# A decoder step on one core: the residual add of the last stage on GpSimd instead of VectorE

## The reference, cut to what matters

```
x = x + g2 * _apply_moe(h2, ...)
y = x * lax.rsqrt(jnp.mean(x * x, axis=-1, keepdims=True) + 1e-6) * final_g
```

## Time and profile before

| | us |
|---|---|
| median of 3 runs | 1414.49 (1413.54 to 1415.04) |
| the profiled execution, its own time | 1411.95 |
| its span in the profile | 1409.3 |
| PE, DVE, ACT, POOL busy in the span | 1237.8, 751.2, 509.1, 187.0 |
| last store of expert rows issued | 1354.03 |
| last stage, from its first load to the end of the span | 1357.96 to 1409.3 |

### The profile page before, as it was taken

The page is one execution under the profiler, slowest core; times in us unless marked ns, Lnnn a source line. Parts: engine busy times, 40 slices in busy tenths (PEclk is TensorE's granted clock), DMA queues, the critical chain, the costliest instruction groups (busy, mean ns, idle before and its releaser), DMA issues.

```text
span 1409.3 us, 18005 instructions
## 1 busy us (share of the span) xinstructions
PE 1237.8 (88%) x6859; PEld 946.1 (67%) x6859; DVE 751.2 (53%) x1417; ACT 509.1 (36%) x862; POOL 187.0 (13%) x169
## 2 busy tenths in 40 slices
PE   3688989899898899999999978996399998999956
PEld 1576767677675788888888867884367766666622
DVE  0665556645656452111111125445679887888827
ACT  1443232323324221111100112111178877878732
POOL 1110000000000000000000001110012253466301
PEclk8899999999999899999999999998589999999978
DMA  9442122231321121111111023223769999999644
GB/s 353 177 155 94 63 100 79 85 137 31 139 80 55 50 114 71 46 45 46 45 45 45 0 90 149 74 78 106 274 225 370 365 368 341 376 359 366 260 194 185
DMA packets 40717, 219.73 MB, mean 156 GB/s; under 512 B 7432, under 2 KB 15056, under 8 KB 27978
## 3 DMA queue, kind: packets, MB, share of 16 engines
q1 hardware_dynamic: 32194, 197.15, 37.5%
q0 software_dynamic: 7536, 18.51, 3.9%
q10 hardware_dynamic: 928, 3.28, 0.6%
HBM read 202.03 MB, written 24.72 MB: 161 GB/s over the span
## 4 chain that ended last, share of the span: by engine, by line
PE 62%; DVE 17%; DMA 14%; issue 3%; ACT 3%; SPq 1%; POOL 0%; ACTq 0%; POOLq 0%; DVEq 0%
PE p L1852 10%; PE p L1944 8%; DMA G<-in_we 8%; PE p L1619 7%; PE p L1856 6%; PE p L1789 3%; PE p L1879 3%; PE psS L1852 3%; PE psS L1879 3%; PE psS L1963 3%; DMA M<-in_x 2%; PE psS L1856 2%; DVE work L1150 2%; PE p L1686 2%; PE p L1697 1%
## 5 line engine op out<-in xcount | busy, mean ns | idle before, releaser
L1619 PE MATMUL p<-A 128*128 128x512 f32 (+3 forms) x1080 | 261.1, 389 | 14.3 <-DVE A L1047 14.3
L1619 PEld LDWEIGHTS p<-A 128*128 128x128 f32 (+1 forms) x1080 | 176.9, 185 | 66.8 <-DVE A L1047 16.2
L1944 PE MATMUL p<-C 128*96 128x512 f32 x768 | 195.0, 406 | 19.4 <-DVE C L1498 19.3
L1944 PEld LDWEIGHTS p<-C 128*96 128x96 f32 x768 | 122.5, 166 | 77.8 <-issue 30.3
L1487 DVE TENSOR_TENSOR C<-G,C 128x2048 fp32r<-128x2048 f32 x64 | 146.2, 2285 | 37.2 <-ACT C L907 37.2
L1302 DVE TENSOR_TENSOR work<-p,work 128x344 f32<-128x344 f32 x36 | 18.6, 517 | 238.4 <-ACT work L843 238.0
L1852 PE MATMUL p<-A,B 128*128 128x344 f32 x864 | 143.0, 323 | 2.0 <-DVE M L1236 2.0
L1852 PEld LDWEIGHTS p<-A,B 128*128 128x128 f32 x864 | 137.3, 188 | 4.4 <-issue 2.2
L907 ACT CAST C<-G 128x2048 fp32r<-128x2048 f32 x64 | 122.5, 1916 | 28.9 <-DMA G<-in_we 23.0
L1963 PE MATMUL psS<-C 128*96 128x512 f32 x384 | 98.3, 406 | 5.4 <-DVE C L1510 5.4
L627 POOL DMA_INDIRECT y_dram<-M,slotY x32 | 87.9, 2746 | 96.4 <-ACT M L936 96.4
(11 more groups left out here) (289 smaller groups left out, 1814.6 us busy)
## 6 DMA issues: line engine op xcount, KB each, us to landing
G<-in_we SPq DMA_DIRECT2D x32, 2048.0 KB, 18.3
G<-in_we SPq DMA_DIRECT2D x32, 1024.0 KB
M<-in_w_ada SPq DMA_DIRECT2D x8, 2048.0 KB, 8.0
M<-in_x SPq DMA_DIRECT2D x18, 512.0 KB, 4.2
M<-in_rope SPq DMA_DIRECT2D x45, 192.0 KB, 2.4
D<-in_w_qkv SPq DMA_DIRECT2D x4, 2048.0 KB, 7.8
F<-in_lift SPq DMA_DIRECT2D x8, 1024.0 KB, 5.1
M<-y_dram SPq DMA_DIRECT2D x8, 1024.0 KB, 11.9
```

The source lines that it names most:

```text
L1619: last = mm(out, x[k][:, t0:t0 + rows], y(k), start=k == 0 and j == 0, stop=k == KD - 1 and j == 2)
L1944: last = mm(up_bank[slot][0:CAP, :], x[:, k, :], kcols(w, k), start=k == 0 and j == 0, stop=k == KD - 1 and j == 2)
```

## The change

The add of the gated expert rows to the residual goes from DVE to POOL; DVE's `finish` follows two tiles behind `combine` instead of one; and `x2_r` is split. `x2_g` now counts gated tiles, which frees PE's banks and releases POOL's add; `x2_r` is counted by that add and still releases ACT's square. POOL's order is add(0), then add(t), rs3(t-1) for t = 1 to 8, then rs3(8); rs3(t) waits for finish(t-2), as `rstd3` has two columns. DVE's wait for its own halves in `combine` is gone. One semaphore, `modT_t`, is taken out and its step counted on `c_step` instead, with the same event and the same waiter, near the start of the program.

```
 CS = {... "cT_r": 4, "mod_t": 5}          # c_step counts modT_t's step too (DVE wait, PE inc)
@@ GpSimd
             def rs3(t):
                 pool.wait_ge(s["x2_sq"], t + 1)
+                if t >= 2:
+                    pool.wait_ge(s["yo_r"], t - 1)
...
+            def add_rows(t):
+                r = P if t < NT else NS
+                x = x1[0:r, t, :]
+                pool.wait_ge(s["x2_g"], t + 1)
+                nc.gpsimd.tensor_tensor(x, x, yg[0:r, t, 0], ALU.add).then_inc(s["x2_r"], 1)
             for t in range(NT + 1):
-                rs3(t)
+                add_rows(t)
+                if t:
+                    rs3(t - 1)
+            rs3(NT)
@@ VectorE
             def combine(t):
...
-                    link.mark(nc.vector.tensor_tensor(y0[:, cols], sum_bank[t % 3][n][0:r], gate[0:r, cols], ALU.mult))
-                link.wait()
-                nc.vector.tensor_tensor(x, x, y0, ALU.add).then_inc(s["x2_r"], 1)
+                    last = nc.vector.tensor_tensor(y0[:, cols], sum_bank[t % 3][n][0:r], gate[0:r, cols], ALU.mult)
+                last.then_inc(s["x2_g"], 1)
...
             combine(0)
-            for t in range(1, NT + 1):
+            combine(1)
+            for t in range(2, NT + 1):
                 combine(t)
-                finish(t - 1)
+                finish(t - 2)
+            finish(NT - 1)
             finish(NT)
@@ TensorE
                 if t >= 3:
-                    pe.wait_ge(s["x2_r"], t - 2)
+                    pe.wait_ge(s["x2_g"], t - 2)
```

More of the change, by code:

```diff
@@ L60 @@
 NL = NG + NE
-CS = {"c_sig": 1, "c_silu": 2, "cT_t": 3, "cT_r": 4}
+CS = {"c_sig": 1, "c_silu": 2, "cT_t": 3, "cT_r": 4, "mod_t": 5}
 SK = {"sq_t": 1, "sq_e": 2, "skT_t": 3, "skT_e": 5}
@@ L333, in build @@
         for n in ("const_in misc_in crow_in c_step ada_in0 ada_in1 ada_in2 ada_w "
-                  "ada_b ada_mm mod_r mod_st modT_t tab_in wq_in0 wq_in1 wq_hi wq_lo wq_free wkv_in kv_hi kv_lo x_in0 x_in1 x_in2 x_in3 rope_in0 rope_in1 x_n x_sq rs_r h_r "
+                  "ada_b ada_mm mod_r mod_st tab_in wq_in0 wq_in1 wq_hi wq_lo wq_free wkv_in kv_hi kv_lo x_in0 x_in1 x_in2 x_in3 rope_in0 rope_in1 x_n x_sq rs_r h_r "
                   "hT_t h_hi h_lo kv_mm k_r v_e kT_t kT_e pj rot v_c kd_r qk_t qk_e att_s nm_r ex_r pn_r pT_e st_u "
@@ L342, in build @@
                   "s2 hs h_a hid_r y_e y_st0 y_st1 y_st2 y_done wd_r ys_mm stab_in yg_in0 yg_in1 yg_in2 yg_in3 yg_in4 yg_in5 yg_in6 yg_in7 yg_in8 "
-                  "x2_r x2_sq rs3_r yo_r out_st0 out_st1").split():
+                  "x2_g x2_r x2_sq rs3_r yo_r out_st0 out_st1").split():
             sem(n)
@@ L1017, in _ @@
             link.wait()
-            dve.wait_ge(s["modT_t"], 1)
+            dve.wait_ge(s["c_step"], CS["mod_t"])
             parts = p2[:, :].rearrange("p (q j r) -> p j q r", q=4, j=4)
@@ L1559, in combine @@
                 gate = G2 if t < NT else G2s
-                y0, x = yg[0:r, t, 0], x1[0:r, t, :]
+                y0 = yg[0:r, t, 0]
                 for n in range(2):
@@ L1647, in _ @@
                 last = nc.tensor.transpose(p2[:, q * P:(q + 1) * P], mod[:, q * P:(q + 1) * P], ident)
-            last.then_inc(s["modT_t"], 1)
+            last.then_inc(s["c_step"], 1)
             kv(0)
```

## The result

The changed kernel takes 1420.22 us (median of 11 runs, 1416.63 to 1421.27), the kernel before 1413.54 (11 runs): ratio 1.0044, 95% interval 1.0036 to 1.0053, so 6.2 us slower (5.1 to 7.5). The forecast was 3.4 us slower, at 1417.9.

What follows compares the result with a forecast made beforehand. DVE was taken as the bound at 3.65 us a tile, PE close behind; POOL rounds of 4.10 us plus the tail end the last norm at 1407.9 instead of 1404.5, so 1414.49 + 3.4 = 1417.9 us, range 1412.8 to 1422.5.

Steps and rivals of the forecast that it cites:

- DVE just slower than PE, so little to win: Last stage: DVE takes 3.65 us a tile, PE 3.43, so relieving DVE can bring only 0.22 us a tile.
- Blocking both ways, one instruction against the other: Final norm and POOL's add, each reading two SBUF tensors, exclude each other; the norm holds the add 1.07 us.
- Gates are free of it: DVE's gates in the last stage read PSUM and one SBUF tensor, so POOL's add does not block them.
- POOL becomes the bound: Last stage: POOL's round is 0.03 + 1.07 + 2.1 + 0.90 = 4.10 us, 0.45 a tile slower than DVE before.
- DVE takes the port first: At each power's end, DVE's norm starts 0.03 us later, ahead of POOL's next add, and holds it 1.07 us.
- POOL gets the port first: Rival, chance 0.12: POOL's add starts before DVE's norm, which waits 2.0 us; rounds 4.5 to 4.6, time 1420.5.
- The first store is no wait any more: Norm 2 comes after tile 0's store has landed, so DVE's 1.9 us wait goes, without gain on the path.
- PE's loads wait for banks late in the stage: Sign: PE's loads stay at 0.43 us until its banks run out, then wait for gates late in the stage.

Runs made afterwards that it cites:

- the changed kernel again: The changed kernel, unaltered, run once more on the same chip as three other kernels: ratio 1.0032 to the kernel before.
- the fill: Kernel before, with POOL filling 128x2048 with zeros, reading nothing, behind each of the first eight powers: ratio 1.0001.

## Why the prediction was right

*DVE just slower than PE, so little to win.* Right. With the blocking gone and the add on POOL, rounds took 3.43 to 3.44 us, PE's pace, where DVE had set 3.65.

*Blocking both ways, one instruction against the other.* Right, and shown by experiments of its own. The sizes read from rows 6 and 7 hold: a norm holds POOL's add off for 0.97 to 1.04 us (1.07 taken), an add holds the norm off for 2.1 (2.0 taken).

*Gates are free of it.* Right: 684 ns in both kernels.

*POOL becomes the bound.* Right, with rounds of 4.46 instead of 4.10. The size was too small, 3.4 us against 6.2, and these terms made it so. The add takes 2.35 us, not the 2.1 that two passes of a copy would: 0.25 x 7 adds in a row (tiles 2 to 8; the power behind the add of tile 1 is still done just before gate 2) = 1.75 us. And the forecast gave every meeting to DVE. In fact the two orders take turns, 4.19 and 4.72 a round. By the forecast's terms with the measured add, a round would be 4.10 + 0.25 = 4.35; the average is 4.46, so 0.11 x 6 = 0.66 us more. Two errors lie in this 0.11: a round with DVE first measures 4.19, so its hand-over, hold and power were taken 0.16 too long (2.00 for 4.19 - 2.35 = 1.84), and the turns add 0.27 to it. In the profile with a short low clock, gate 2 was also done 0.3 us later after PE's start than forecast. Together 3.4 + 1.75 + 0.66 + 0.3 = 6.1, against 6.2 timed and 6.0 between the two profiles with a short low clock (47.6 - 41.6). (By the Trainium skill, GPSIMD Engine Reference, section 3.1 Elementwise, half of its 4497 ns at 2048 columns is an estimate of 2.25 us for the add, nearer than the 2.1 taken; the trace has 2.35.)

*DVE takes the port first.* Wrong as reasoned, and in half of the meetings right by luck. The forecast had the power release the norm and the add together, and the norm start first. Wherever the power does release both, it is the add that starts first, by 0.06 to 0.07 us (1382.61 against 1382.67, 1391.52 against 1391.59, 1400.43 against 1400.49): it stands right behind the power in POOL's own queue and starts before the power's row has ended, so the gap of 0.07 us that the forecast gave POOL does not exist there. DVE came first in the other rounds for a reason that was forecast for tile 2 alone: there DVE is the late one, the norm stands right behind the gates in DVE's own queue, and the add waits for these same gates by semaphore (the norm at 1387.17, the add at 1387.33 with 0.60 us of idle time ended by L1575). The rival "POOL gets the port first" had the right reason for every second round, and its time, 1420.5, and its round, 4.5 to 4.6, lie nearer to what was measured than the forecast's; that they came so near is in part luck too, since it also took 2.1 us for the add and expected no turns.

*The first store is no wait any more.* Right: the norms of the eight prompt tiles in the changed kernel wait for POOL's power alone, 8.0 us in all.

*PE's loads wait for banks late in the stage.* Not seen: DVE's gates fell behind by less than three tiles. It was worth nothing in the sum.

## What to carry to other kernels

In these runs, moving an elementwise operation with two SBUF inputs from VectorE to GpSimd took its time from VectorE without a price only where VectorE's work beside it read at most one tensor in SBUF (the gates, and the norm with its gain in PSUM); look in the trace for what VectorE will be doing at that moment, and for a small GpSimd row that is longer beside it than elsewhere. If the two must meet, put one of VectorE's operands in PSUM, if banks are free: here that took back all of a 6 us loss. And first compare the paces: where the next engine is 0.2 us a tile behind the bound, even a free offload can bring only that, less than the blocking cost here.

## What the runs showed of the hardware that was not expected

*Which of the two comes first alternates.* With 0.06 us between the two starts, the one that came first was served whole. The turns come from the program's own order. When the norm has been held, DVE is behind, and its next norm follows the gates in its own queue, ahead of the add that waits for these gates by semaphore. When the add has been held, POOL is behind, DVE has its gates done and idles, and the power releases POOL's next add, in POOL's own queue, just ahead of the norm. All seven meetings, tiles 2 to 8, took turns like this in both profiles of the changed kernel.

*PE's low clock at the start of the stage has two lengths.* The rows give the second window of PE, from 3 to 5 us after its first multiplication: stretch, us, busy, granted clock, DMA share, GB/s. First the changed kernel, then the changed kernel again, then the control with the gain in PSUM and the add on DVE:

```profile
1367.25:1369.25 2.00, 2.00 (x3) 0.50 1.01 426
```
```profile
1365.91:1367.91 2.00, 2.00 (x5) 0.82 1.00 422
```
```profile
1367.50:1369.50 2.00, 2.00 (x3) 0.50 1.02 430
```

PE had been idle for 10.6 us before the stage. It starts at 0.50 of its clock (1.2 GHz), and the granted clock goes to the full one (2.4 GHz) 3.0 to 3.7 us later in some executions and 5.2 to 6.0 in others, read in stretches of 0.5 us, with the same multiplications. Over 13 profiles the short one came in 5 and the long one in 8, both with the add on DVE and with it on POOL, so the change alone does not decide it; what does was not found. In the changed kernel the stage took 47.6 us with the short one and 48.5 with the long one. Where DVE sets the pace it cost nothing (41.4 us beside the fill and 41.5 with the gain in PSUM, both with the long one, against 41.6), since DVE then waited less for the first store (0.5 to 0.7 us instead of 1.9).
